# Head group D: values as the stationary operand of the product with the probabilities, two heads in two column groups, division moved to the probabilities

## What is computed

```
s = einsum(q, k) * scale + bias          # bias: ALiBi penalty; masked keys -1e30
p = softmax(concat([s, sink]))[..., :-1] # the sink only adds to the sum
od = einsum(p, v)                        # D_HEADS 8, D_KV_HEADS 2, HEAD_DIM 64
y = concat([oc, od]) @ w_out             # oc comes from group C
```

## Time and profile before

| | |
|---|---|
| median of 3 runs | 3544.19 us |
| the runs | 3557.42, 3544.19, 3541.68 us |
| profiled execution | span 3550.5 us; the profile gives no other time of it |
| PE | busy 3300.5 us, 93% |
| DVE | busy 1479.8 us, 42% |
| ACT | busy 1051.1 us, 30% |
| mean granted clock of PE | 0.953 |

### The profile page before, as it was taken

How to read it: one execution, slowest core, us unless ns; L and a number is a source line. 1 busy time by engine, 2 the same in 40 slices (tenths; PEclk the granted TensorE clock), 3 DMA queues, 4 the chain that set the end, 5 groups by cost and what they waited for, 6 DMA issues and landing times. The chain is left out here.

```text
span 3550.5 us, 49644 instructions
## 1 busy us (share of the span) xinstructions
PE 3300.5 (93%) x17488; PEld 2767.6 (78%) x17488; DVE 1479.8 (42%) x2714; ACT 1051.1 (30%) x2417; POOL 585.6 (16%) x352
## 2 busy tenths in 40 slices
PE   5999999999989999999999989989897999999997
PEld 4777777766579999999966556655456999999996
DVE  4233366567153343333441434434324343443335
ACT  3333355454132221222210033334404222222222
POOL 2111111110032222222300000000003223222220
PEclk8999999899999999999999989978898999999998
DMA  2111110000101111111011100000001111111111
GB/s 85 37 37 37 37 39 30 30 22 16 51 30 43 48 43 43 43 49 43 31 47 36 32 10 8 4 4 12 24 29 39 47 43 42 49 43 43 43 42 51
DMA packets 52798, 127.65 MB, mean 36 GB/s; under 512 B 11760, under 2 KB 19968, under 8 KB 52640
## 3 DMA queue, kind: packets, MB, share of 16 engines
q1 hardware_dynamic: 44160, 108.33, 9.2%
q0 software_dynamic: 5312, 16.80, 1.4%
q10 hardware_dynamic: 3168, 0.18, 0.1%
HBM read 111.52 MB, written 13.76 MB: 35 GB/s over the span
## 5 line engine op out<-in xcount | busy, mean ns | idle before, releaser
L1053 PE MATMUL ps<-hh,wh 128*128 128x384 f32 (+1 forms) x2112 | 697.5, 330 | 38.4 <-POOL hl L113 33.0
L1053 PE MATMUL ps<-hl,wh 128*128 128x384 f32 (+1 forms) x2112 | 697.2, 330 | 0.0
L1053 PE MATMUL ps<-hh,wl 128*128 128x384 f32 (+1 forms) x2112 | 696.4, 330 | 0.0
L1180 POOL TENSOR_TENSOR wl<-raw,wh 128x1024 fp32r<-128x1024 f32 x132 | 330.1, 2501 | 1123.6 <-ACT wh L1106 1123.6
L1053 PEld LDWEIGHTS ps<-hh,wh 128*128 128x128 f32 x2112 | 400.9, 190 | 42.6 <-issue 42.6
L1053 PEld LDWEIGHTS ps<-hh,wl 128*128 128x128 f32 x2112 | 401.0, 190 | 0.0
L1053 PEld LDWEIGHTS ps<-hl,wh 128*128 128x128 f32 x2112 | 399.4, 189 | 0.0
L1223 DVE TENSOR_SCALAR gates<-u,par 128x1090 f32<-128x1090 f32 x88 | 74.6, 848 | 772.6 <-ACT tail L1131 772.6
L225 PE MATMUL pot<-hh_mix,wh_mix 128*128 128x384 f32 (+1 forms) x576 | 220.0, 382 | 30.5 <-ACT q_next L261 16.1
L1106 ACT ACTIVATE wh<-raw 128x1024 fp32r<-128x1024 f32 x132 | 138.8, 1051 | 341.0 <-PE pot L1072 193.3
L225 PE MATMUL pot<-hl_mix,wh_mix 128*128 128x384 f32 (+1 forms) x576 | 195.3, 339 | 0.0
(11 more groups left out here) (224 smaller groups left out, 5774.4 us busy)
## 6 DMA issues: line engine op xcount, KB each, us to landing
raw<-in_ffn_w SPq DMA_DIRECT2D x132, 512.0 KB, 3.2
w<-in_w SPq DMA_DIRECT2D x64, 256.0 KB, 2.5
w<-in_w SPq DMA_DIRECT2D x12, 512.0 KB, 3.6
w<-in_w_out SPq DMA_DIRECT2D x16, 256.0 KB, 2.6
strip<-in_bias POOLq DMA_DIRECT2D x5, 640.0 KB, 4.1
x<-in_x SPq DMA_DIRECT2D x4, 768.0 KB, 9.3
out_y<-x SPq DMA_DIRECT2D x2, 1536.0 KB, 6.3
out_bv<-vt POOLq DMA_DIRECT2D x4, 512.0 KB, 3.0
```

The source lines that it names most:

```text
L1053: mm = e.matmul(bank[:, 0:b - a], w[:, n % 3, k * P:(k + 1) * P], x[:, k, a:b], start=k == 0 and first, stop=k == KT - 1 and w is m.wl)
L1180: e.tensor_tensor(m.wl[:, n % 3, :], m.raw[:, n % 3, :], m.wh[:, n % 3, :].bitcast(F32), ALU.subtract).then_inc(self.low, 1)
```

## The change

Group D alone is changed; A, B and C keep their paths. Three things change together:

1. Division. `ve_scale` adds exp(sink) to a unit's row sums, takes the reciprocal, and multiplies the unit's probabilities wk (up to 128 x 256) with it in place, for every unit in the step's list behind the front of the next unit. PE's transposes of the unit now wait for this (`normed`) instead of for `probs`. `ve_normalise` and otok are no longer used in D.
2. Product with the values. `pe_out_pair` works both heads of a tile together, in even steps: vtok_d (64 columns) is the stationary operand and pt streams with 128 columns; head 0 goes to partitions 0 to 63 of po, head 1 to 64 to 127, alternating. po then already has the orientation that o wants. pt gets four places, one per unit modulo 4.
3. Leaving PSUM. `sc_keep` copies po into o with one ACT instruction per tile, in odd steps, and counts `kept`. The nine otok transposes and their PSUM fillings are gone.

```diff
@@ -370,11 +371,12 @@
                 mine.append(len(self.uses))
                 self.uses.append((u, tuple(range(g, min(g + 4, nb)))))
             self.unit_uses.append(mine)
-            if u >= 2 and u % 2 == 0:
+            if kind != "D" and u >= 2 and u % 2 == 0:
                 self.out_use[u // 2 - 1] = len(self.uses)
                 self.uses.append(("o", (u // 2 - 1,)))
-        self.out_use[NQT - 1] = len(self.uses)
-        self.uses.append(("o", (NQT - 1,)))
+        if kind != "D":
+            self.out_use[NQT - 1] = len(self.uses)
+            self.uses.append(("o", (NQT - 1,)))
...
@@ -464,9 +468,12 @@
                 self.pe_scores(e, j, step + 1)
             if step == -1 and st:
                 self.pe_turn_v(e, j)
-            if 1 <= step <= UNITS:
+            if self.kind == "D":
+                if step >= 2 and step % 2 == 0:
+                    self.pe_out_pair(e, j, step // 2 - 1)
+            elif 1 <= step <= UNITS:
                 self.pe_out(e, j, step - 1)
-            if step >= 3 and step % 2:
+            if self.kind != "D" and step >= 3 and step % 2:
                 self.pe_turn_out(e, j, (step - 3) // 2)
...
@@ -535,7 +542,7 @@
 
     def pe_turn(self, e, j, u):
         m, nq = self.m, self.nq(u)
-        e.wait_ge(self.probs, j * UNITS + u + 1)
+        e.wait_ge(self.normed if self.kind == "D" else self.probs, j * UNITS + u + 1)
...
+
+    def pe_out_pair(self, e, j, t):
+
+        m, nq = self.m, self.nq(2 * t)
+        self.wait_back(e, j, self.unit_uses[2 * t + 1][-1] + 1)
+        if t:
+            e.wait_ge(self.kept, j * NQT + t)
+        m.apart(e)
+        bl = self.blocks(2 * t)
+        for i, (k, kw) in enumerate(bl):
+            for hh in range(2):
+                at = 256 * ((2 * t + hh) % 4) + P * i
+                mm = e.matmul(m.po[HEAD * hh:HEAD * hh + HEAD, 0:nq], m.vtok_d[0:kw, k // P, HEAD * hh:HEAD * hh + HEAD],
+                              m.pt[0:kw, at:at + nq], start=i == 0, stop=i == len(bl) - 1, skip_group_check=True)
+        mm.then_inc(self.out, 1)
...
-            if step >= 3 and step % 2 == 1:
+            if kind == "D":
+                if step >= 3 and step % 2:
+                    self.sc_keep(e, j, (step - 3) // 2)
+            elif step >= 3 and step % 2 == 1:
                 self.sc_output(e, j, (step - 3) // 2)
...
+    def sc_keep(self, e, j, t):
+        m = self.m
+        nq, q0 = self.nq(2 * t), self.qcol(2 * t)
+        e.wait_ge(self.out, j * NQT + t + 1)
+        m.apart(e)
+        e.activation(m.o[:, bass.ds(j + self.otile, 1), q0:q0 + nq], m.po[:, 0:nq], ACT.Copy).then_inc(self.kept, 1)
...
+        at = 256 * (u % 4) if self.kind == "D" else 0
+        pt = m.pt[:, at:]
...
@@ -706,7 +740,10 @@
                 self.ve_front(e, j, step + 1)
             if step == -1:
                 self.read_v(e, "v", j)
-            if step >= 1 and step % 2 == 0:
+            if kind == "D":
+                if 0 <= step < UNITS:
+                    self.ve_scale(e, j, step)
+            elif step >= 1 and step % 2 == 0:
                 self.ve_normalise(e, j, step // 2 - 1)
...
+
+    def ve_scale(self, e, j, u):
+        m = self.m
+        nq, w, s8 = self.nq(u), self.keys(u)[1] - self.keys(u)[0], u % 8
+        total = m.rowsum[0:nq, s8:s8 + 1]
+        e.wait_ge(self.probs, j * UNITS + u + 1)
+        e.tensor_tensor(total, total, m.esink[0:nq, s8:s8 + 1], ALU.add).then_inc(self.inv, 1)
+        e.wait_ge(self.inv, j * 2 * UNITS + 2 * u + 1)
+        e.reciprocal(total, total).then_inc(self.inv, 1)
+        e.wait_ge(self.inv, j * 2 * UNITS + 2 * u + 2)
+        wk = m.wk[0:nq, u % 2, 0:w]
+        e.tensor_scalar(wk, wk, total, None, ALU.mult).then_inc(self.normed, 1)
```

More of the change, by code:

```diff
@@ L358, in __init__ @@
         self.out, self.inv, self.normed = sem("out"), sem("inverse"), sem("normed")
+        self.kept = sem("output_kept")
         self.qcopied = sem("q_copied")
@@ L437, in wait_all @@
         e.wait_ge(self.back_s, PAIRS * self.use_by.count("s"))
+        if self.kind == "D":
+            e.wait_ge(self.kept, PAIRS * NQT)
     def pairs(self, e, body, last=False):
@@ L664, in read_turned @@
         if nq == P:
-            ops.append((m.pt[:, P * bl[0]:P * (bl[-1] + 1)], bank[:, 0:P * len(bl)]))
+            ops.append((pt[:, P * bl[0]:P * (bl[-1] + 1)], bank[:, 0:P * len(bl)]))
         else:
@@ L668, in read_turned @@
             v = lambda x: x.rearrange("p (b f) -> p b f", f=P)[:, :, 0:nq]
-            ops.append((v(m.pt[:, P * bl[0]:P * (bl[0] + n)]), v(bank[:, 0:P * n])))
+            ops.append((v(pt[:, P * bl[0]:P * (bl[0] + n)]), v(bank[:, 0:P * n])))
             if len(full) < len(bl):
-                ops.append((m.pt[0:HEAD, P * (bl[0] + n):P * (bl[0] + n) + nq], bank[0:HEAD, P * n:P * n + nq]))
+                ops.append((pt[0:HEAD, P * (bl[0] + n):P * (bl[0] + n) + nq], bank[0:HEAD, P * n:P * n + nq]))
         for dst, src in ops:
```

## The result

| | before | after |
|---|---|---|
| median | 3547.76 us (4 runs) | 3654.16 us (4 runs, 3644.24 to 3660.45) |
| ratio | | 1.030, 95% interval 1.0276 to 1.0324 |
| span of the profiled execution | 3550.5 us | 3648.5 us |
| D, from its windows | 210 us | 319 us |

The change costs 106 us, 3%. In the two profiled executions D is 109 us longer and all the rest 11 us shorter.

A forecast was written before the change was run, and what follows sets the result against it. PE was busy over nine tenths of most of D, partly at the lower clock; the change would make each step wait on DVE. Terms +57, +16, -5 and -6 gave +62 on 3544.2: 3606 us, range 3580 to 3672.

The forecast's parts named there:

- likeliest case: D's steps lengthened by PE's wait for the scaling, clock share unchanged: 3606 us, own range 3590 to 3625, chance 0.60.
- rival B: Clock in D stays low because new steps have PE gaps: between 3650 and 3694 us, chance 0.25.
- the prediction's own signs: In D's profile: steps staying at 2.5, clock 0.50 for most of D, or scaling far off 0.36 would prove it wrong.
- On DVE the scaling stands behind the next front, PE's transposes wait for it, a step is the whole chain: Each D step: 3.61 us against 2.48 or 2.70 at clock 1.00; 5.11 against 3.47 at 0.50.
- The chain at 1.00 is 3.61 us: D's step from scores over DVE front, division and PE transposes to the next scores: 3.61 us at clock 1.00.
- The sum: +62 us: All of D: steps +57 at 1.00 and +16 at 0.50, narrow units -5, pairs' ends -6.
- The clock stays as it was: D's sum kept the earlier clock share: 59 of 210 us at 0.50, 14 step triples there, 54 at 1.00.
- gapless sixth steps: D steps with paired product and two output projection products: gapless at 0.50, may bring clock 1.00 back.
- The pairs' ends give back 6 us: At each head pair's end in D the otok transpose chain goes: 1.47 us saved a pair, 5.9 in all.
- The paired product costs and brings nothing at 1.00: PE's eight passes in every second D step, at most 1.16 us, hide in the wait: no gain or loss.
- Rival C: In D the transpose need not wait for the scaling, so only gains of 6 and 17 us remain: 3521, chance 0.04.
- Rival D: D's wait real but cheaper: shorter DVE gaps, scaling 0.21, clock 1.00 earlier; +40 us, 3584, chance 0.11.

The follow-up runs named there:

- e1: Changed kernel without D's add, reciprocal and scaling, transposes waiting for the exponential as before (D's results left undivided): 3537.34 us, ratio 0.9983 to the kernel before.
- e4: Changed kernel with the same division instructions, but scaled probabilities written where nobody reads and transposes waiting only for the exponential: 3533.75 us, ratio 0.9974 to the kernel before.
- e5: Changed kernel with the division of each unit put ahead of the next unit's front on DVE: 3550.20 us, ratio 1.0016 to the kernel before.
- e2: Kernel before with only the division moved behind the next front and transposes waiting for it; product and otok transpose kept: 3676.29 us, ratio 1.0369.
- e3: Changed kernel with a useless PE product between scores and transposes in eleven steps of 18: 3588.74 us, ratio 1.0126 to the kernel before.
- e7: Changed kernel with division ahead of the next front and all output projection products ahead of the transposes: 3542.90 us, ratio 0.9980 to the kernel before.
- e8: The e7 kernel plus three useless PE products around each meeting between pairs: 3530.21 us, ratio 0.9943 to the kernel before.

## Why the prediction was right, and where not

The direction and the range (3580 to 3672) held; the figure, 3606, did not: the loss is 106 us, not 62, and 3654 lies outside the likeliest case's own 3590 to 3625. The range held because it reached over the near part of rival B, to which I gave 0.25, and B at its 3650 is what came: by the prediction's own signs (the clock at 0.50 for most of D) its main case was wrong.

- *On DVE the scaling stands behind the next front, PE's transposes wait for it, a step is the whole chain.* Right, and shown from four sides: without the division (e1), with DVE's work and no wait (e4), with the other order (e5) the loss is gone; with the division alone (e2) it is all there.
- *The chain at 1.00 is 3.61 us.* It is 3.38. The scaling itself was well sized (0.36 against 0.35); too long were scores to front (0.98 against 0.91), scaling to transpose (0.21 against 0.12; I took it from the end of a pair) and transposes to next scores (1.07 against 1.02). At 0.50: 5.11 expected, 4.79 measured, and half of the difference is the last of these (2.06 against 1.90).
- *The sum: +62 us.* The same clock share as before was taken. At about that share (e3) the wait costs 46 us, so the term was too large by a third. The shorter chain accounts for it: with the measured steps (3.38, 3.38 and 3.28 us at 1.00; 4.79, 4.79 and 5.07 at 0.50) the prediction's own sum gives about 43.
- *The clock stays as it was.* This is the step that failed. It was put as a rival and left out of the sum. The earlier trace rows showed that 1.00 came back out of steps without a gap, and the new steps have one; I counted the gapless sixth steps against it and gave B only 0.25. The trace shows such steps bring 1.00 back now and then, and the next waiting steps lose it again, as in the spell from 2397 to 2403. The price is 63 us, more than the wait itself. The Trainium skill ("TensorE: Matmul & The Clock Gate", section on depth-cycling of the PSUM queue) says that PE which often idles briefly swings between its two clocks, and this trace agrees: ten short spells at 1.00 in D, between stretches at 0.50 of up to 82 us. The measured 3654 lies at the lower end of the 3650 to 3694 that I gave for it.
- *The pairs' ends give back 6 us.* Right in the changed kernel: 0.2 us for 1.67 and 2.04 for 3.49 at the pair's end shown. In the faster variants (e1, e5) PE waits longer for the next queries, as far as the trace tells for POOL's reload of strip and sink.
- *The paired product costs and brings nothing at 1.00.* It is hidden in the wait, as said. Its eight passes take 0.66 us at 1.00, where at most 1.16 had been allowed, and 1.12 at 0.50; before, four passes took 0.58 at 1.00. The Trainium skill (same page, Part 3) says that products in different column groups run side by side, and this trace agrees: the passes start in pairs 7 ns apart. What the product is worth where no wait covers it stays small: e1 and e7 are both 0.2% under the kernel before, with intervals that reach to 0.3 and 0.4%.
- *Rival C, not slower*, needs the scaling ready before the next front. The order of the change did not do that; e5 does, and its 3550 us are not slower by much, but neither e5 nor e7 (3543) comes to C's 3521.
- *Rival D, a cheaper wait*, was right in its first part: the wait alone cost 46 us, not 62, through shorter gaps in the chain. The scaling was not cheaper, and 1.00 did not come earlier.

## What to carry to other kernels

When an operation is moved between two engines' steps, look at what stands ahead of it in its own engine's list and at what its new reader has queued behind itself; here its own 0.35 us did not matter, but its place behind the next unit's front made every step a full round trip, and swapping two lines cured nearly all of it. Price a wait on PE twice: once for the time, and once for the clock it may lose; here the second was the larger, and it shows only if the sum is also made at the lower level. If a gap on PE can't be closed, fill it with work that belongs there, and without such work a useless product can pay.

## What the runs showed of the hardware

- Adding useless passes made the changed kernel some 62 us faster (e3: clock in D 0.92 for 0.58), and twelve useless products around the pairs' meetings made e8 13 us faster than e7 (0.99 for 0.82).
- At 0.50, PE busy for 68 of 82 us, with gaps of 0.65 and 1.70 us in most of its steps, did not bring 1.00 back. At 1.00, PE busy for about 50 of 64 us held it in e3, where the gaps were 0.2 to 0.9 us; in the changed kernel steps with gaps of 1.1 and 1.7 us lost it.
- In e8 PE still stands idle for 2.1, 1.6 and 2.7 us at the three meetings, between useless products; the clock stayed at 1.00 through the first two and fell at the third.
- Products of two column groups run side by side: in the trace their passes start in pairs 7 ns apart, eight passes of 128 columns in 0.66 us at 1.00, 1.12 at 0.50.
